# One core, two decoder layers: the feed-forward's 22 tiles in four groups (4, 4, 6, 8) in place of three (6, 8, 8), and weight sums issued in other stages

## The chip, the core and the metric

The program runs on one core of one Trainium2 chip, in one launch. The metric is the device time of that launch in microseconds. TensorE multiplies, VectorE (DVE) and ScalarE (ACT) prepare operands and empty PSUM, GpSimd (POOL) computes a few rows and issues accumulating DMAs, SyncE (SP) issues the loads of the weights.

## The reference, cut to what matters

Two layers on 592 tokens (a prompt of 528, and 8 samples of 8). Each layer is a mixer, a layer norm, a gated feed-forward with a causal convolution of width 3, and a layer norm. The change concerns the feed-forward:

```python
def _conv_ffn(x, buf, w_up, conv_w, conv_b, w_down):
    u, v = jnp.split(x @ w_up, 2, axis=-1)
    uc, new_buf = _causal_dwconv(u, buf, conv_w, conv_b)
    h = jax.nn.gelu(uc.astype(jnp.float32)) * v.astype(jnp.float32)
    return h.astype(x.dtype) @ w_down, new_buf.astype(buf.dtype)
...
    for layer in range(DEPTH):
        if layer % 2 == 0:
            m, s_ret, s_hgrn = _mixer_ret_hgrn(x, pos, segments, s_ret, s_hgrn, layer, p)
        else:
            m, h_lru, buf_lru = _mixer_rglru(x, h_lru, buf_lru, p)
        x = _layernorm(DEEPNORM_ALPHA * x + m, ...)
        f, nb = _conv_ffn(x, buf_ffn[layer], ...)
        x = _layernorm(DEEPNORM_ALPHA * x + f, ...)
```

D_MODEL is 1024 (8 tiles of 128) and D_FF is 2816 (22 tiles of 128), all in float32.

## The kernel before, in words

**Products.** Channels lie on the partitions and tokens on the columns. Every float32 operand is held as a high and a low part, and each 128 x 128 block of a weight takes three matmuls on a half of the tokens (`products`: high by high, high by low, low by high; lines 773 to 775), 296 columns wide in layer 0 and 290 or 288 in layer 1. A unit is one output tile's weights. An up-projection unit (u or v of one feed-forward tile) takes 8 blocks x 2 halves x 3 = 48 matmuls; a down-projection unit takes 6 matmuls for each tile of its group.

**Groups.** The 22 tiles of a feed-forward are worked off in groups (`GROUPS`): the tiles of a group are made one after another, and then eight down units (d0 to d7, one for each output tile) add the group's part to Y. `ffn_order` writes this order. The first `SINGLE` tiles are made one at a time, as unit u and unit v. From there on, two tiles are made together (`pair_of_tiles`): for each of u and v, seven half-sized products of sums of weights and sums of inputs take the place of eight, so that the u or the v of two tiles takes 7 x 4 x 3 = 84 matmuls. A block of four units (a and b for u, p and q for v) makes the two tiles.

**Sums of weights.** They are made in DRAM (`weight_sums`) by `sum_step`: POOL issues eight DMAs in a chain for each group that holds pairs, four of them plain and four accumulating, each behind the landing of the one before. Before the change there are two such groups in a layer, of 8 pair units each, 2048 KB a step. The two of layer 0 are made in the first stage (one step of each after each of the eight heads), the two of layer 1 behind the layer norms numbered 1 and 2 (0 is the one after layer 0's mixer, 3 the last).

**Sums of inputs.** `input_sums(k)` (DVE), their high parts (ACT) and their low parts (DVE) for k = 0 to 3 stand behind the tiles j = 1 to 4.

**The stream of weights.** SP loads the units in order into four buffers `raw` (a pair unit needs two loads, and waits for its group's sums). ACT copies the high part (line 1149, `weights_hi`), DVE subtracts it to make the low part (line 1621, `weights_lo`); each of these has four places. Which unit is prepared in which step is written out (`weights_at`, `block_of_pairs`). SP may refill a `raw` buffer when its low part is made. SP, ACT and DVE each take their work in program order, so that one late load holds what stands behind it.

**PSUM.** Two accumulators alternate between units. A down unit may begin when `add_tile` on DVE (line 1841 where the tile is scaled by alpha, line 1843 otherwise) has added what its accumulator held to Y. A gated tile h is finished by DVE and ACT: rows of the last product, the gate, the high part on ACT, the low part on DVE (`h_lo`); a down unit waits for each h tile in the order in which it reads them.

**The recurrence's rates.** `lambda_rows` (lines 2137 to 2151) computes a few numbers for layer 1's mixer with 27 small DVE instructions; in the kernel before they stand behind the first down unit's `add_tile` of layer 0's first group.

Of the kernel before, what the change touches and what calls it, by code (L numbers as in the profile page):

```python
# [23 lines left out]
P = 128  # L24
# [14 lines left out]
FT = DFF // P  # L39
GROUPS = [6, 8, 8]  # L40
ALPHA = float((2.0 * 2) ** 0.25)
# [19 lines left out]

SINGLE = 6
SUM_STEPS = [(0, "a21", False), (1, "a11", False), (0, "a22", True), (1, "a21", True),
# [29 lines left out]
def mixer_order():  # L93

    order = [("r", 0), ("r", 1)]
    for m in range(2, KT, 2):
# [20 lines left out]
            ("output", -1), ("sample", 1), ("mean", 1), ("moment", 3), ("steps", 3), ("norm", 5)]  # L117
R_LAST = {"sample": 0, "mean": 0, "moment": 2, "steps": 2, "norm": 4}


# [57 lines left out]
def wid(u):  # L178

    return (T - off(u)) // 2  # L180
# [9 lines left out]
PER_LAYER = len(PAIRS) // 2  # L190
PER_GROUP = PER_LAYER // (len(GROUPS) - 1)
RAWS = 4
# [140 lines left out]
def trunk(nc, xT, xP, weights, gates, params, consts, tables, s_ret, s_hgrn, yT, ret_out, hgrn_out, small_out):  # L333
    with ExitStack() as ctx:
# [264 lines left out]
        def _(sp):  # L599
# [6 lines left out]
            def load_weights(u, i):  # L606
# [10 lines left out]
                n = PAIRS.index(u - second(u))  # L617
                sp.wait_ge(w_sums[n // PER_GROUP], 16 * len(SUM_STEPS))
                if second(u):
# [43 lines left out]
        def _(pool):  # L663
# [14 lines left out]
            def sum_step(group, step):  # L678

                first, last = slice(0, HALF), slice(HALF, 2 * HALF)  # L680
                n = group * PER_GROUP
                units = weights[PAIRS[n]:PAIRS[n] + 2 * PER_GROUP].rearrange("(n t) p c -> t p n c", t=2)
                sums = W_SUMS[n:n + PER_GROUP].rearrange("n p c -> p n c")
                to, source, add = SUM_STEPS[step]
                source = {"a11": units[0][:, :, first], "a12": units[0][:, :, last], "a21": units[1][:, :, first],
                          "a22": units[1][:, :, last], "s1": sums[:, :, 0:HALF],
                          "s2": sums[:, :, 2 * HALF:3 * HALF]}[source]
                if step:
                    pool.wait_ge(w_sums[group], 16 * step)
                dst = sums[:, :, to * HALF:to * HALF + HALF]  # L690
                if add:
                    pool.dma_start(dst, source, accum_op=ALU.add).then_inc(w_sums[group], 16)
                else:
                    pool.dma_start(dst, source).then_inc(w_sums[group], 16)
# [6 lines left out]
            for n in range(2 * HEADS):  # L701
# [4 lines left out]
                if n + 2 < 2 * HEADS:  # L706
                    pool.wait_ge(st_out, 32 * (n + 1))
                    load_states(n + 2)
                for group in range(2):
                    sum_step(group, n)  # L710
# [22 lines left out]
            for ln in range(3):  # L733
# [16 lines left out]
                for m in range(KT):  # L750
                    low_row(ln, 1, m)
                if ln:
                    for step in range(len(SUM_STEPS)):
                        sum_step(1 + ln, step)
            for i in range(3):
# [14 lines left out]
        def _(pe):  # L770
# [6 lines left out]
            def gemm(u, hi, lo, k_ready=None, k0=0, both=False, side=None, per=1):  # L777
# [3 lines left out]
                for k in range(n):  # L781
# [19 lines left out]
                    if side:  # L801
                        side(u, k)
                        if both:
                            side(u + 1, k)

            def half_product(u, half, k, hi, lo, signal=None, third=None, norm=None):
# [271 lines left out]
            def ffn(layer):  # L1078
                ub = U_FFN0 if layer == 0 else U_FFN1
                for i, (kind, j, g, first) in enumerate(FFN):  # L1080
# [6 lines left out]
                    elif i > N_FFN - 4:  # L1087
                        pass
                    elif kind == "d":
                        gemm(ub + i, hhi, hlo, h_lo, FT * layer + first)  # L1090
                    elif i == 0:
# [41 lines left out]
        def _(act):  # L1133
# [204 lines left out]
            def ffn(layer):  # L1338
# [88 lines left out]
                for i, (kind, j, g, first) in enumerate(FFN):  # L1427
# [40 lines left out]
                    else:  # L1468
                        if layer == 0 and g == 0 and j == 0:
                            done(act.activation(lam[:, 0:KT], par("lru_lambda", 0, KT), ACT.Abs))  # L1470
# [135 lines left out]
        def _(dve):  # L1606
# [357 lines left out]
            def ffn(layer):  # L1964
# [127 lines left out]
                for i, (kind, j, g, first) in enumerate(FFN):  # L2092
# [33 lines left out]
                    elif kind == "d":  # L2126
                        add_tile(u, j, g == 0, 2 * layer + 1 if g == len(GROUPS) - 1 else None)
                        if layer == 0 and g == 0 and j == 0:
                            lambda_rows()
# [274 lines left out]
```

## Time and profile before

| what | value |
|---|---|
| median of 3 runs | 1366.58 us (1365.96 to 1368.08) |
| the profiled execution's own time | 1366.96 us |
| its span, first to last instruction | 1365.2 us |
| TensorE busy in the span | 1347.3 us, 99%, 9900 matmuls |
| VectorE busy | 952.8 us, 70% |
| ScalarE busy | 723.0 us, 53% |
| GpSimd busy (DMA issues not counted) | 137.7 us, 10% |
| granted TensorE clock | 0.997 of full |

A matmul's row has a length of about 300 ns, since the fill and the drain are in it, while the next one starts some 135 ns later. So the time of a stretch is read from starts, or from a count of matmuls in a window, never from the sum of lengths. The clock at full grant is the 2.4 GHz level. The sequencers' rows (SPq) mark when a load is issued, not when it lands.

### The profile page before, as it was taken

The page shows a single profiled execution, that of the slowest core. Times are in us where ns is not written, and L with a number is a line of the kernel's source. Part 1 is how long each engine was busy: PE and PEld are TensorE (multiplying, and loading weights), DVE is VectorE, ACT ScalarE, POOL GpSimd, SP SyncE. Part 2 cuts the span into 40 slices and gives each one's busy share as a digit, 9 for nine tenths or more (in the row PEclk, how much of TensorE's full clock was granted, in tenths as well). Part 3 has the DMA queues.
Part 4 walks back from the last instruction along what each step waited for, and adds up shares of the span by engine and source line. Part 5 has one row for each costly group of instructions (what it writes and reads, how often), then busy time and mean ns, then how long its engine had stood idle before and what let it go on. Part 6 is the DMA issues. An engine that isn't in the chain of part 4 may idle for free.

```text
span 1365.2 us, 24924 instructions
## 1 busy us (share of the span) xinstructions
PE 1347.3 (99%) x9900; PEld 1319.2 (97%) x9900; DVE 952.8 (70%) x1499; ACT 723.0 (53%) x1137; POOL 137.7 (10%) x146
## 2 busy tenths in 40 slices
PE   9999999999999999999999999999999999999996
PEld 8999998999999999999999999999999999999996
DVE  6656665665887568835886778888784688358865
ACT  5443634454674256623673578646652466246734
POOL 0020111101310000000000420123300000000002
PEclk9999999999999999999999999999999999999998
DMA  8185597859622345523554268752598955235512
GB/s 322 58 263 173 126 229 210 224 152 305 149 65 74 90 133 169 171 78 116 163 170 139 63 202 218 201 136 94 185 201 216 255 169 177 80 115 163 171 62 86
DMA packets 80899, 217.49 MB, mean 159 GB/s; under 512 B 6928, under 2 KB 9232, under 8 KB 80528
## 3 DMA queue, kind: packets, MB, share of 16 engines
q1 hardware_dynamic: 52560, 138.83, 31.7%
q0 software_dynamic: 27648, 76.03, 23.1%
q8 instruction: 78, 1.28, 0.4%
q10 hardware_dynamic: 576, 1.05, 0.2%
q14 instruction: 37, 0.30, 0.1%
HBM read 208.25 MB, written 74.74 MB: 207 GB/s over the span
## 4 chain that ended last, share of the span: by engine, by line
PE 87%; DVE 7%; ACT 3%; DMA 1%; issue 1%; SPq 0%; DVEq 0%; ACTq 0%
PE PS L773 27%; PE PS L774 26%; PE PS L775 26%; DMA raw<-weights 1%; PE PS L981 1%; DVE Y L1916 1%; PE PS L911 1%; DVE Y L1904 1%; PE PS L934 1%; PE PS L974 1%; DVE S L2245 1%; PE PS L953 1%; PE PS L1115 0%; DVE wlo L1621 0%; PE PS L957 0%
## 5 line engine op out<-in xcount | busy, mean ns | idle before, releaser
L773 PE MATMUL PS<-xhi,whi 128*128 128x296 f32 (+1 forms) x1536 | 469.6, 306 | 1.1 <-DVE wlo L1627 0.9
L774 PE MATMUL PS<-xlo,whi 128*128 128x296 f32 (+1 forms) x1536 | 458.1, 298 | 0.0
L775 PE MATMUL PS<-xhi,wlo 128*128 128x296 f32 (+1 forms) x1536 | 457.9, 298 | 0.0
L1149 ACT ACTIVATE whi<-raw 128x1024 fp32r<-128x1024 f32 (+2 forms) x256 | 253.8, 994 | 200.5 <-PE PS L775 192.4
L1621 DVE TENSOR_TENSOR wlo<-raw,whi 128x1024 fp32r<-128x1024 f32 (+2 forms) x256 | 294.2, 1152 | 66.1 <-ACT whi L1149 56.7
L773 PEld LDWEIGHTS PS<-xhi,whi 128*128 128x128 f32 x1536 | 290.3, 189 | 5.4 <-issue 2.2
L774 PEld LDWEIGHTS PS<-xlo,whi 128*128 128x128 f32 x1536 | 290.9, 189 | 1.3
L775 PEld LDWEIGHTS PS<-xhi,wlo 128*128 128x128 f32 x1536 | 289.8, 189 | 0.0
L773 PE MATMUL PS<-hhi,whi 128*128 128x296 f32 (+2 forms) x864 | 258.1, 299 | 0.4 <-DVE Y L1841 0.4
L774 PE MATMUL PS<-hlo,whi 128*128 128x296 f32 (+2 forms) x864 | 256.9, 297 | 0.0
L775 PE MATMUL PS<-hhi,wlo 128*128 128x296 f32 (+2 forms) x864 | 256.3, 297 | 0.0
L773 PEld LDWEIGHTS PS<-hhi,whi 128*128 128x128 f32 x864 | 162.7, 188 | 1.5 <-issue 0.8
L774 PEld LDWEIGHTS PS<-hlo,whi 128*128 128x128 f32 x864 | 162.6, 188 | 0.4
L775 PEld LDWEIGHTS PS<-hhi,wlo 128*128 128x128 f32 x864 | 162.6, 188 | 0.0
L775 PE MATMUL PS<-XT,wlo 128*128 128x296 f32 (+1 forms) x512 | 152.6, 298 | 0.0
L773 PE MATMUL PS<-XT,whi 128*128 128x296 f32 (+1 forms) x512 | 151.9, 297 | 0.0
L774 PE MATMUL PS<-XT,whi 128*128 128x296 f32 (+1 forms) x512 | 151.6, 296 | 0.0
L774 PEld LDWEIGHTS PS<-XT,whi 128*128 128x128 f32 x512 | 96.7, 189 | 0.0
L773 PEld LDWEIGHTS PS<-XT,whi 128*128 128x128 f32 x512 | 96.6, 189 | 0.0
L775 PEld LDWEIGHTS PS<-XT,wlo 128*128 128x128 f32 x512 | 96.3, 188 | 0.0
L725 POOL TENSOR_TENSOR S<-S,Y 128x296 f32<-128x296 f32 (+2 forms) x12 | 9.9, 821 | 707.2 <-DVE Y L1871 660.5
L1843 DVE TENSOR_TENSOR Y<-PS,Y 128x592 f32<-128x592 f32 (+1 forms) x24 | 18.4, 766 | 77.4 <-PE PS L775 77.4
(283 smaller groups left out, 1662.8 us busy)
## 6 DMA issues: line engine op xcount, KB each, us to landing
raw<-weights SPq DMA_DIRECT2D x118, 512.0 KB, 4.4
weight_sums<-weights POOLq DMA_DIRECT2D x24, 2048.0 KB, 16.8
raw<-weights SPq DMA_DIRECT2D x96, 256.0 KB, 3.4
weight_sums<-weight_sums POOLq DMA_DIRECT2D x8, 2048.0 KB, 11.1
raw<-weight_sums SPq DMA_DIRECT2D x64, 256.0 KB, 3.4
raw<-weight_sums SPq DMA_DIRECT2D x32, 512.0 KB, 4.1
raw<-weights SPq DMA_DIRECT2D x16, 384.0 KB, 3.2
Y<-xP SPq DMA_DIRECT2D x8, 296.0 KB, 7.3
```

The source lines that it names most:

```text
L773: pe.matmul(dst, wh, h, start=first, stop=False, skip_group_check=onto)
L774: pe.matmul(dst, wh, lo, start=False, stop=False, skip_group_check=onto)
L775: return pe.matmul(dst, wl, h, start=False, stop=last, skip_group_check=onto)
L911: mm = pe.matmul(out, s(KK, c * P, c * P + P), queries, start=True, stop=True)
L934: mm = pe.matmul(SC[:, b * P:b * P + P], kT[0:w, b, :], v[0:w, b, :], start=True, stop=True)
L953: mm = pe.matmul(OT[:, a:a + P], v[:, PLACE[b], :], s(at, a, a + P), start=True, stop=(b == 0))
L974: mm = pe.matmul(OT[:, 512 * c:512 * c + 512], kT[r:r + 32, BLK, :], VX[r:r + 32, :, :].rearrange("p b v -> p (b v)"), start=True, stop=Tr ...
L981: mm = pe.matmul(PS[:, 4 + half, 0:HT], const("mean_h"), s(row, half * HT, half * HT + HT), start=True, stop=True)
L1149: act.activation(high(u, i)[:, 0:n], raw_of(u, i), ACT.Copy).then_inc(w_hi, 1)
L1621: tt(low(u, i)[:, 0:n], raw_of(u, i), high(u, i)[:, 0:n].bitcast(F32), ALU.subtract).then_inc(w_lo, 1)
L1843: done(tt(y, a, y, ALU.add), free[u % 2], u // 2 + 1)
L1904: done(tt(y, y, over_rows(4 + half, n), ALU.subtract))
```

## The change

`GROUPS` becomes 4, 4, 6, 8 and `SINGLE` 4, so that tiles 4 to 21 are made in pairs: nine blocks in a layer where there were eight, and 32 down units where there were 24. The groups with pairs are now of 4, 6 and 8 pair units, six groups in all. The first two down units of each group are interleaved (`two_down_tiles`): both take all but the last one (first group) or two h tiles, then both take the rest. The steps of the weight sums are dealt out anew: the first seven steps of the groups 0 and 1 in the heads' stage, their eighth behind layer norm 0; groups 2 and 3 and half of 4 after the first two pair products of layer 0; the rest behind the layer norms 1 and 2. The fourth of the input sums moves behind the down units d1, d2 and d3 of the first group, and `lambda_rows` behind d0 of layer 0's third group.

```diff
-GROUPS = [6, 8, 8]
+GROUPS = [4, 4, 6, 8]
...
-SINGLE = 6
+SINGLE = 4
...
+ALL_STEPS = range(len(SUM_STEPS))
+SUMS_BEHIND = [[(0, 7), (1, 7)],
+               [(4, step) for step in ALL_STEPS[4:]] + [(5, step) for step in ALL_STEPS[:2]],
+               [(5, step) for step in ALL_STEPS[2:]]]
+SUMS_BEHIND_PAIRS = [(2, step) for step in ALL_STEPS] + [(3, step) for step in ALL_STEPS] + [(4, step) for step in ALL_STEPS[:4]]
...
-PER_GROUP = PER_LAYER // (len(GROUPS) - 1)
+GROUP_OF = [layer * (len(GROUPS) - 1) + FFN[u - base][2] - 1 for layer, base in enumerate((U_FFN0, U_FFN1))
+            for u in PAIRS if base <= u < base + N_FFN]
...
-                sp.wait_ge(w_sums[n // PER_GROUP], 16 * len(SUM_STEPS))
+                sp.wait_ge(w_sums[GROUP_OF[n]], 16 * len(SUM_STEPS))
...
-                for group in range(2):
+                for group in range(2 if n < 2 * HEADS - 1 else 0):
                     sum_step(group, n)
...
-                if ln:
-                    for step in range(len(SUM_STEPS)):
-                        sum_step(1 + ln, step)
+                for group, step in SUMS_BEHIND[ln]:
+                    sum_step(group, step)
+                if ln == 0:
+                    pool.wait_ge(prod, 2 * PRODUCTS)
+                    for group, step in SUMS_BEHIND_PAIRS:
+                        sum_step(group, step)
...
+            def two_down_tiles(u, late, k0):
+
+                n = unit_tiles(u)
+                for ks in (range(n - late), range(n - late, n)):
+                    for i in range(2):
+                        for k in ks:
+                            pe.wait_ge(h_lo, k0 + k + 1)
+                            cols = slice(k * P, k * P + P)
+                            if k == 0:
+                                weights_ready(pe, u + i)
+                                pe.wait_ge(free[(u + i) % 2], (u + i) // 2)
+                            for half in range(2):
+                                t = span(half, off(u + i))
+                                mm = products(acc[(u + i) % 2][:, half, 0:wid(u + i)], high(u + i)[:, cols],
+                                              low(u + i)[:, cols], hhi[:, k, t], hlo[:, k, t], k == 0, k == n - 1)
+                            if k == n - 1:
+                                mm.then_inc(full[(u + i) % 2], 1)
...
+                    elif kind == "d" and j == 0:
+                        two_down_tiles(ub + i, 2 if g else 1, FT * layer + first)
                     elif kind == "d":
-                        gemm(ub + i, hhi, hlo, h_lo, FT * layer + first)
+                        if j > 1:
+                            gemm(ub + i, hhi, hlo)
...
-                        if layer == 0 and g == 0 and j == 0:
+                        if g == 0 and j == 2:
+                            input_sums_hi(KT // 2 - 1)
+                        if layer == 0 and g == 2 and j == 0:
...
-                        if layer == 0 and g == 0 and j == 0:
+                        if g == 0 and j == 1:
+                            input_sums(KT // 2 - 1)
+                        elif g == 0 and j == 3:
+                            input_sums_lo(KT // 2 - 1)
+                        if layer == 0 and g == 2 and j == 0:
                             lambda_rows()
```

How DVE's instructions stand around `lambda_rows`. Before the change they follow the first `add_tile` (L1841) of layer 0's first down units:

```order
L1621 TENSOR_TENSOR wlo<-raw,whi 128x768 [waits weights_hi,h_lo_ready]
L1841 SCALAR_TENSOR_TENSOR Y<-Y,PS 128x592 [waits acc0_full]
L2137 TENSOR_SCALAR lam<-lam 128x8 [waits lambda_exp,acc0_free]
L2138 RECIPROCAL lam<-lam 128x8 [waits dve_step]
L2139 TENSOR_TENSOR lam<-lam 128x8 [waits dve_step]
```

After the change they follow the first `add_tile` (now L1876) of the third group, which also has down units of six tiles; behind them come the low part of d3's weights and d1's `add_tile`, which frees the accumulator for d3:

```order
L1654 TENSOR_TENSOR wlo<-raw,whi 128x768 [waits weights_hi,h_lo_ready]
L1876 TENSOR_TENSOR Y<-PS,Y 128x592 [waits acc0_full]
L2174 TENSOR_SCALAR lam<-lam 128x8 [waits lambda_exp,acc0_free]
L2175 RECIPROCAL lam<-lam 128x8 [waits dve_step]
```

```order
L2188 TENSOR_SCALAR lam<-W 128x16 [waits dve_step]
L1654 TENSOR_TENSOR wlo<-raw,whi 128x768 [waits weights_hi,half_biases_ready]
L1876 TENSOR_TENSOR Y<-PS,Y 128x592 [waits acc1_full]
L1654 TENSOR_TENSOR wlo<-raw,whi 128x768 [waits weights_hi,acc1_free]
L1876 TENSOR_TENSOR Y<-PS,Y 128x592 [waits acc0_full]
```

The neighbours on DVE are the same; what moved is that TensorE now runs d0 and d1 interleaved ahead of this place. On POOL, the steps that now stand between the layer norms 0 and 1 are these (the middle number of the shape is the number of pair units):

```order
L701 DMA weight_sums<-weights 128x8x512 [waits weight_sums_of_group2]
L699 DMA weight_sums<-weights 128x8x512 [waits weight_sums_of_group2] x2
L701 DMA weight_sums<-weight_sums 128x8x512 [waits weight_sums_of_group2]
L699 DMA weight_sums<-weights 128x8x512 [waits weight_sums_of_group2]
L701 DMA weight_sums<-weight_sums 128x8x512 [waits weight_sums_of_group2]
L699 DMA weight_sums<-weights 128x8x512 [waits weight_sums_of_group2]
L701 DMA weight_sums<-weights 128x4x512
L701 DMA weight_sums<-weights 128x4x512 [waits weight_sums_of_group3]
```

L701 is a plain step and L699 an accumulating one. Before the change no step stands there.

## Rows read from the trace of the kernel before

**Rows 1.** The page: busy time of the engines (us, share, instructions); granted clock in 40 slices.
```profile
PE 1347.3 (99%) x9900; PEld 1319.2 (97%) x9900; DVE 952.8 (70%) x1499; ACT 723.0 (53%) x1137; POOL 137.7 (10%) x146
...
PEclk9999999999999999999999999999999999999998
```

**Rows 2.** TensorE's waits: line, releaser, us in total, times, longest.
```profile
PE PS L773 <- DVE Y L1841: 1.0, 3, 0.6
PE PS L773 <- DVE wlo L1627: 0.9, 1, 0.9
```

**Rows 3.** Windows: stretch, us, PE busy (matmuls begun or running), clock, DMA share, GB/s.
```profile
388.96:447.87 58.91, 58.91 (x435) 1.00 0.25 74
447.87:487.19 39.32, 39.32 (x291) 1.00 0.36 107
487.19:578.33 91.14, 91.14 (x675) 1.00 0.53 157
...
973.62:1031.16 57.54, 57.54 (x434) 1.00 0.89 242
...
1069.28:1159.29 90.01, 90.01 (x674) 1.00 0.64 185
```

**Rows 4.** DVE's timeline, layer 0's d0 and d1: start, us, engine, line, op [idle before].
```profile
452.97 0.77 DVE L1841 SCALAR_TENSOR_TENSOR Y<-Y,PS 128x592 f32<-128x592 f32 x1 [0.94 <-PE PS L775]
...
460.12 0.77 DVE L1841 SCALAR_TENSOR_TENSOR Y<-Y,PS 128x592 f32<-128x592 f32 x1
```

**Rows 5.** TensorE and DVE, timeline, behind two interleaved units of layer 0's mixer.
```profile
325.65 0.30 PE L775 MATMUL PS<-hhi,wlo 128*128 128x296 f32 x1
326.16 0.37 PE L773 MATMUL PS<-hhi,whi 128*128 128x296 f32 x1 [0.21 <-DVE Y L1841]
...
325.25 0.77 DVE L1841 SCALAR_TENSOR_TENSOR Y<-Y,PS 128x592 f32<-128x592 f32 x1 [1.04 <-PE PS L775]
```

**Rows 6.** DVE's timeline behind tile 3 (both layers), and a low part 512 wide.
```profile
420.92 1.22 DVE L1621 TENSOR_TENSOR wlo<-raw,whi 128x1024 fp32r<-128x1024 f32 x1
...
424.61 0.22 DVE L2121 TENSOR_TENSOR S<-PS,S 128x64 f32<-128x64 f32 x1
...
1008.60 0.22 DVE L2121 TENSOR_TENSOR S<-PS,S 128x64 f32<-128x64 f32 x1
...
488.20 0.69 DVE L1621 TENSOR_TENSOR wlo<-raw,whi 128x512 fp32r<-128x512 f32 x1
```

**Rows 7.** ACT, DVE and TensorE, timeline, in front of layer norm 0.
```profile
340.23 1.06 ACT L1149 ACTIVATE xhi<-raw 128x1024 fp32r<-128x1024 f32 x1 [4.57 <-DMA raw<-weights]
...
342.47 0.77 DVE L1841 SCALAR_TENSOR_TENSOR Y<-Y,PS 128x592 f32<-128x592 f32 x1
...
343.38 0.37 PE L773 MATMUL PS<-hhi,xhi 128*128 128x296 f32 x1 [0.61 <-DVE Y L1841]
```

**Rows 8.** DVE's timeline behind the pairs of a group: two h tiles' low parts.
```profile
580.29 1.65 DVE L2043 TENSOR_TENSOR hlo<-S,hhi 128x592 fp32r<-128x592 f32 x2
```

**Rows 9.** POOL's last sum step; DMA in 1067 to 1088; last two lines: the page's.
```profile
1066.43 1.52 POOL L692 DMA_DIRECT2D weight_sums<-weights  x1 [9.20 <-DMA weight_sums<-weight_sums]
...
q1 hardware_dynamic: 1514, 3.25, 43.6%
...
weight_sums<-weights POOLq DMA_DIRECT2D x1, 2048.0 KB, 21.8
raw<-weights SPq DMA_DIRECT2D x5, 256.0 KB, 7.1
...
weight_sums<-weights POOLq DMA_DIRECT2D x24, 2048.0 KB, 16.8
raw<-weights SPq DMA_DIRECT2D x96, 256.0 KB, 3.4
```

**Rows 10.** SP: first load of a pair block behind six-tile units; POOL: start at layer norm 1.
```profile
461.90 0.33 SPq L628 DMA_DIRECT2D raw<-weights  x1
...
766.15 0.82 POOL L725 TENSOR_TENSOR S<-S,Y 128x296 f32<-128x296 f32 x1 [381.77 <-DVE Y L1871]
```

More of the change, by code:

```diff
@@ L680, in sum_step @@
                 first, last = slice(0, HALF), slice(HALF, 2 * HALF)
-                n = group * PER_GROUP
-                units = weights[PAIRS[n]:PAIRS[n] + 2 * PER_GROUP].rearrange("(n t) p c -> t p n c", t=2)
-                sums = W_SUMS[n:n + PER_GROUP].rearrange("n p c -> p n c")
+                n, count = GROUP_OF.index(group), GROUP_OF.count(group)
+                units = weights[PAIRS[n]:PAIRS[n] + 2 * count].rearrange("(n t) p c -> t p n c", t=2)
+                sums = W_SUMS[n:n + count].rearrange("n p c -> p n c")
                 to, source, add = SUM_STEPS[step]
```

## The prediction

> **What bounds the kernel now.** I read the page first: TensorE is busy 99% of the span at the 2.4 GHz level in all but the last slice [rows 1]. Then its waits: of the 18 us in which it is idle, the list of waits names only a handful, each under 2 us, and of the kind that concerns this change there are 1.0 and 0.9 us in all [rows 2]. In the feed-forwards the windows show it busy for their whole length [rows 3], and the timeline has no pause between two products there. So the feed-forwards are bound by the number of matmuls, and every other engine matters only where it becomes late. That makes two kinds of term: matmuls saved, and new waits at places that had none.
>
> **Matmuls.** In layer 0, nine single units (432 matmuls; the count in the row has three more that were still running) take 58.91 us, 6.546 each. Four blocks of pairs (672 matmuls) take 91.14, 22.79 a block. In layer 1 the same are 57.54/9 = 6.393 and 90.01/4 = 22.50 [rows 3]. The change turns two single tiles (four units) of each layer into one block: 26.18 - 22.79 = 3.40 and 25.57 - 22.50 = 3.07. **-6.5 us.** The down units have the same matmuls as before in all (8 x 22 tiles), only cut into 32 units for 24; six-tile units run at 39.32/288 = 136.5 ns a matmul and the single units at 136.4 [rows 3], so a unit's start costs nothing.
>
> The rows show 136 ns from start to start at 296 columns. The Trainium skill ("TensorE: Matmul & The Clock Gate", Part 1) gives N / 2.4 GHz plus about 2.5 ns for back-to-back matmuls, an estimate of 126 ns. By it the term would be -6.0; the trace disagrees, and I go by the rows.
>
> **What pays for the smaller groups.** DVE gets 16 more `add_tile`s of 0.77 us, ACT and DVE six more copies of 1024 columns each (a block prepares seven half units for u and v each, against four for single tiles). These 20 us of DVE work lie beside TensorE: DVE is busy 70%, and they fall into stretches in which TensorE has 3.3 us for a four-tile down unit (24 x 136.5 ns) while DVE needs 0.77 plus 0.69 for the low part. They cost nothing as long as nothing is late. So I looked at each place where something is later than before relative to TensorE.
>
> **lambda_rows.** Before, d0's `add_tile` begins at 452.97, the 27 small instructions, d3's low part and d1's `add_tile` follow, and that last one ends at 460.12 + 0.77 = 460.89, that is 7.92 us after the first began [rows 4]. DVE began 0.2 after d0 was full (447.87 + 4.92 = 452.79 [rows 3]), and TensorE begins 0.14 after a release (326.02 to 326.16 [rows 5]), so d3 may start 0.2 + 7.92 + 0.14 = 8.26 us after d0 is full. Before, d1 and d2 of 4.92 us each lay between, 9.8 us: 1.6 to spare. Now d1 is all but two tiles done when d0 is full. Only 12 matmuls (1.64) and d2 (4.92) are left, 6.56 us. The third group's down units are of six tiles as well, and the instructions behind are the same. TensorE waits 8.26 - 6.56 = **+1.7 us**, in layer 0 alone. ACT's part of it is early enough (d0 lasts longer now).
>
> **d2 behind d0 in the first group.** There only one tile is left for last, so d0 is full 0.8 us ahead of d1, and d2 needs d0's accumulator after those six matmuls. This case is in the trace: the first two units of the output projection are interleaved in the same way, and TensorE's start-to-start there is 0.51 instead of 0.14, with DVE's 0.77 as releaser [rows 5]: 0.37. Twice: **+0.7 us.** In the other groups two tiles are left, 1.64 us, and 0.2 + 0.77 + 0.14 = 1.1 fits.
>
> **d1 behind v3.** Two interleaved units also need both accumulators sooner: d1 begins after three tiles of d0, 2.46 us (layer 1: 2.38), instead of a whole unit of 4.9. v3's accumulator is free when DVE's last gate instruction ends. Tile 3 carries input sums, and there that end is 424.83, 3.14 us after the unit's (388.96 + 5 x 6.546 = 421.69 [rows 3]); in layer 1 it is 1008.82, 3.23 after 973.62 + 5 x 6.393 = 1005.59 [rows 3, 6]. The low part in between shrinks from 1.22 to 0.69 [rows 6]. With the 0.14 that gives 2.75 and 2.84 against 2.46 and 2.38: 0.3 + 0.46, **+0.8 us**. Bounds: 0 and, without the narrower low part, 1.8.
>
> **Behind the pairs of a four-tile group** only four down tiles' halves (3.28 us) hide the last two h tiles, where six (4.9) did. In the trace the two low parts run from 580.29 to 581.94 [rows 8]; the first is ready 2.8 us and the second 3.6 us after TensorE's end at 578.33 [rows 3], against needs at 3.28 and 4.10. With 0.14 it fits by 0.3. I take 0, with 1 us as the upper end for both layers together, should DVE be late there.
>
> **Layer norm 0.** Before, a load of weights that landed at 340.2 kept ACT idle for 4.57 us. DVE's `add_tile` stood behind that load's low part and started only at 342.47, and TensorE began a unit at 343.38, 0.77 later than a product's pace of 0.135 allows (its row counts 0.61 as idle) [rows 7]. The load stood behind five loads of x rows while POOL's two last steps of 2048 KB, which the change moves behind the layer norm, were moving. Without them I expect it 1 us or more earlier: **-0.8 us**, bounds -0.8 and 0.
>
> **Sum:** -6.5 + 1.7 + 0.7 + 0.8 - 0.8 = -4.1 (-4.0 before rounding). The profiled execution took 1366.96, 0.4 more than the median of 1366.58. Its sum gives 1362.9, and against the median I predict **1362.5 us**, 0.3% less.
>
> **Weight sums beside the pairs.** This is the doubtful cover. The sums of groups 2, 3 and 4 now run while TensorE works on pairs, when SP's queue alone keeps the DMA engines busy to 0.53 [rows 3]. The trace has 21 us of this overlap, in layer 1: the last accumulating step took 21.8 us, SP's loads of 256 KB landed in 7.1 us where the page's median is 3.4, SP's queue held 43.6% of the engines and moved 3.25 MB in 21 us, 155 GB/s [rows 9] against 157 needed [rows 3]. TensorE did not pause. So the overlap is at the edge, and a step's 20 us are borne by what is prepared ahead. Between two accumulating steps stands a plain one of about 10 us (9.20 waited plus the issue [rows 9]) in which it catches up, except once, where both lie mostly on down units. I take 0.
>
> **Are the sums in time?** Group 2's eight steps take four times 10.1 and four times 16.8 to 21.8 [rows 9], 108 to 128 us. By the terms above the first two pair products end near 471, so they land by 579 to 599. Tile 14's pairs start near 627, and SP issues their first load some 25 us ahead (461.90 for 487.19 [rows 10]), at 602. It fits, barely. POOL ends its list near 710 (at worst 780, if the smaller steps were no shorter) and is wanted at layer norm 1, near 762 (766.15 before, less the sum [rows 10]).
>
> **The rivals.**
> A. *The new waits stay covered* (DVE's order gives more than I see). Then only -6.5 - 0.8 are left: 1359.3 us. For it: no pause in 790 us of feed-forward. Against it: rows 4 and 5 carry the two main waits. 0.15.
> B. *SP's queue falls behind beside the sums; slower than before.* The accumulating steps cover some 110 us of pair stages in layer 0. If SP's queue got half of the engines where it needs 0.53, each us would lose 6%: +6.5, hence 1369. It decides from landings of about 9 us on: a buffer is refilled every four loads, 11.4 us, of which ACT and DVE take 1.06 and 1.22 [rows 6, 7] with a short wait between. The trace has 7.1 [rows 9], and nothing shows what a second such step does. 0.09.
> The Trainium skill ("DMA: Bandwidth & Descriptors", Queues, rings and completion order) says that each DMA engine takes turns between the queues with work, a packet at a time, whatever waits on them. By that rule SP's loads get no precedence; rows 9 agree.
> C. *Group 2's sums or POOL are late.* SP, then ACT, DVE and TensorE wait in turn for tile 14, or layer norm 1 does. Steps 5 us longer than the longest would put it 20 us past 602, against about 15 of reserve: +5, hence 1367.5. 0.05.
> D. *The boundaries cost about double* (h tiles of the four-tile groups, lateness on DVE from late loads, no gain at layer norm 0): +2 to +3, hence 1365. 0.15.
> The forecast keeps 0.56.
>
> **How the numbers follow.** A measurement of this kernel tells 0.2%, 2.7 us, from no change: the border is 1363.8. Faster holds A and 0.51 of the forecast's 0.56: 0.66. Within 0.2% are the forecast's rest, D and a part of C: 0.22. Slower: B and the rest of C, 0.12. The range from 1359.5 to 1367.0 spans the forecast with its bounds, D and most of A, and leaves out B and half of C.
>
> **What would show it.** Right: TensorE has 9852 matmuls; blocks take 22.8 and 22.5 us; TensorE waits once for 1.7 us for `add_tile` in the third group of layer 0, twice for 0.2 to 0.4 in front of d2, twice in front of d1 in the first groups, and no longer at 343. Wrong: a wait on weights' low parts inside the pair blocks of layer 0 (B), SP idle for the sums of group 2 (C), or waits on h tiles behind the second group (D).

## The result, and the profile after

| what | before | after |
|---|---|---|
| median of 19 runs each | 1366.93 us (1365.96 to 1368.19) | 1372.98 us (1368.13 to 1382.21) |
| ratio, 95% interval | | 1.0044 (1.0035 to 1.0054) |
| the profiled execution's own time | 1366.96 us | 1373.03 us |
| its span | 1365.2 us | 1371.1 us |

The change makes the kernel 0.4% slower, where I had forecast 0.3% faster. The time lies outside the range, 6 us above its upper end, and beyond rival B's 1369 too. The profile is of an execution close to the median, so its pauses can be read as the usual ones.

The page of the changed kernel, against [rows 1] and the end of [rows 9]:

```profile
PE 1345.0 (98%) x9852; PEld 1313.2 (96%) x9852; DVE 980.5 (72%) x1555; ACT 734.4 (54%) x1165; POOL 152.3 (11%) x162
...
q1 hardware_dynamic: 57168, 141.98, 31.8%
q0 software_dynamic: 30976, 84.41, 25.9%
...
raw<-weights SPq DMA_DIRECT2D x140, 256.0 KB, 4.3
```

TensorE has the 9852 matmuls that the change promises, 48 fewer. They should have taken 6.5 us of busy time away, and only 2.3 are gone: a matmul's row is 300 ns long where the next one starts after 136, and the first row behind a pause is longer still, so a part of each pause counts as busy. Idle time went from 17.9 us to 26.1. The median landing of SP's loads of 256 KB went from 3.4 to 4.3 us over the whole run, which looks harmless. A median over 140 loads hides the few that matter (13 of them in the stretch that is looked at below).

TensorE's waits, against [rows 2]:

```profile
PE PS L783 <- DVE S L2048: 3.0, 4, 1.5
PE PS L783 <- ACT S L1404: 2.5, 4, 1.0
PE PS L783 <- DVE wlo L1660: 2.0, 2, 1.6
PE PS L783 <- DVE Y L1876: 1.6, 1, 1.6
...
PE PS L783 <- DVE S L2154: 0.3, 1, 0.3
```

The last two rows are waits that the prediction named: `lambda_rows`, and d1 behind v3 in layer 1. Those in front of d2 are too short for a row of their own, and so is d1's in layer 0; they are read from starts below. The third row lies in the first 10 us of the program, with the first products of all. The first two are new and were not named: instructions that empty the accumulators of pairs (L2048 on DVE, L1404 on ACT). They are not slow themselves; they stand behind something. The windows say where. They begin and end with the first matmuls of units or blocks, as in [rows 3]; the last two are of layer 1. Columns: stretch, us, busy time and count of PE, PEld, DVE, ACT and POOL, clock, DMA share, GB/s:

```profile
421.61:448.55 26.94, 26.67 (x195) 26.24 (x194) 19.62 (x28) 9.07 (x14) 0.00 (x0) 1.00 0.43 129
520.34:591.96 71.62, 69.13 (x506) 68.41 (x505) 54.44 (x83) 43.08 (x73) 5.64 (x5) 1.00 0.98 270
633.06:725.90 92.84, 91.86 (x674) 91.20 (x673) 74.22 (x112) 60.73 (x100) 8.50 (x8) 1.00 0.94 262
1035.78:1084.15 48.37, 46.35 (x338) 45.20 (x337) 36.56 (x56) 28.19 (x50) 2.42 (x2) 1.00 0.78 225
1110.38:1177.89 67.51, 67.51 (x506) 67.51 (x505) 55.17 (x85) 43.65 (x73) 0.00 (x0) 1.00 0.52 162
```

The clock is at full grant in all of them, so it has no part in this. The last row is the measure: three blocks of pairs of layer 1 with no sums beside them take 67.51 us, 22.50 each, as before. The fourth holds two blocks and takes 48.37 instead of 45.0. The second holds three blocks of layer 0 and takes 71.62 instead of 3 x 22.79 = 68.4, the third four and takes 92.84 instead of 91.1 (from 91.14 in [rows 3]). In these three the DMA engines are busy to 0.78 to 0.98, where the pairs alone took 0.53 before [rows 3]. Taken block by block from the starts of the matmuls, the pauses inside blocks add up to 5.0 us in layer 0 and 3.4 in layer 1, where the interleaved d0 and d1 of the second group, with DVE late, lose another 0.8 behind the fourth window: **9.2 us** in all. My sum without them was -4.0, which gives +5.2. Measured between the two profiled executions is +6.1, and 0.8 of that is a later start of the first products, ahead of everything that the change touches (the third row of waits).

### One pause, followed back

The pause of 1.8 us at 566, in the second of the three blocks from 520 to 592 us, engine by engine (timelines of ACT, DVE and TensorE):

```profile
563.14 1.06 ACT L1180 ACTIVATE whi<-raw 128x1024 fp32r<-128x1024 f32 x1 [3.24 <-DMA raw<-weight_sums]
...
564.30 1.23 DVE L1654 TENSOR_TENSOR wlo<-raw,whi 128x1024 fp32r<-128x1024 f32 x1 [2.43 <-ACT whi L1180]
565.45 0.45 DVE L2048 TENSOR_TENSOR S<-S,PS 128x296 f32<-128x296 f32 x1
...
565.96 0.41 PE L783 MATMUL PS<-XT,whi 128*128 128x296 f32 x1 [1.53 <-DVE S L2048]
...
567.92 1.06 ACT L1180 ACTIVATE whi<-raw 128x1024 fp32r<-128x1024 f32 x1 [2.38 <-PE PS L785]
```

ACT waits 3.24 us for a load, which landed 9.7 us after SP had issued it at 553.41. DVE waits for ACT's high part, 2.43 us. The instruction that frees the accumulator stands behind the low part in DVE's order, and TensorE waits for that. So the list of waits names a short instruction that empties an accumulator, where the cause is a late load three steps up. The next high part starts at 567.92. Its row names TensorE, whose product ended at 567.86; its load landed at the same moment, 12.8 us after SP had issued it at 555.03, so that either alone would have held it. What ACT does behind a late high part (L1404, which empties an accumulator) is the second row of the list of waits.

What ended ACT's idle time before its high parts, over blocks of pairs of layer 0. Changed kernel, 520 to 592 us:

```profile
  DMA raw<-weight_sums: 6.4, 3
  DMA raw<-weights: 6.2, 4
  PE PS L785: 4.8, 4
```

The kernel before, 520 to 577 us, has one row:

```profile
  PE PS L775: 9.8, 12
```

Before, ACT waited for TensorE alone, that is for a place to write to: it was ahead. Now more than half of its waiting is for loads. And the DMA of the same stretch of the changed kernel:

```profile
q0 software_dynamic: 3475, 9.08, 55.5%
q1 hardware_dynamic: 4615, 10.24, 42.7%
...
weight_sums<-weight_sums POOLq DMA_DIRECT2D x2, 2048.0 KB, 11.5
weight_sums<-weights POOLq DMA_DIRECT2D x2, 2048.0 KB, 20.3
raw<-weights SPq DMA_DIRECT2D x13, 256.0 KB, 8.2
...
raw<-weight_sums SPq DMA_DIRECT2D x8, 256.0 KB, 8.7
```

SP's queue (q1) holds 42.7% of the engines, against 43.6% in the stretch from which I argued [rows 9], so that reading was right. It moves 10.24 MB in 72 us, 142 GB/s, against the 157 that pairs need [rows 3]: 10% short. The landings of 8.2 to 8.7 us are near the 9 from which rival B was said to decide, and as a median, so that half are longer.

The mean share hides how a step begins. The accumulating step issued at 549.69, in two stretches of the changed kernel's DMA, 553.5 to 556.5 and 557 to 565 us (queue, packets, MB, share; SP's loads issued in it, count, KB, median landing):

```profile
q0 software_dynamic: 257, 0.53, 107.9%
...
raw<-weight_sums SPq DMA_DIRECT2D x2, 256.0 KB, 10.1
raw<-weights SPq DMA_DIRECT2D x1, 256.0 KB, 12.8
...
q0 software_dynamic: 489, 1.00, 72.1%
q1 hardware_dynamic: 471, 0.87, 35.9%
```

For 3 us SP's queue moved no packet at all, though four of its loads were outstanding by 555.1, among them the two of the pause above; without the sums a load's first packets move within 1 us of its issue (after_no_sums, issued at 549.47). From then on the queues moved about as many packets each. The other steps beside pairs begin with 1 to 3 such us as well, plain ones too (541 to 543.5: 233 packets against none), and when a step's last packets are through, SP's queue has the engines alone for some 2 us (549.7 to 552: 382 packets against none). The Trainium skill ("DMA: Bandwidth & Descriptors", Queues, rings and completion order) lets each DMA engine take turns between the queues by packet; 557 to 565 us agrees, with 489 packets against 471, the first 3 us of the step do not, and no run here shows why.

POOL's timeline shows the plain step in which SP was to catch up:

```profile
538.46 0.92 POOL L701 DMA_DIRECT2D weight_sums<-weight_sums  x1 [21.14 <-DMA weight_sums<-weights]
549.69 1.52 POOL L699 DMA_DIRECT2D weight_sums<-weights  x1 [10.31 <-DMA weight_sums<-weight_sums]
```

It took 10.9 us as expected (issued 538.46, landed 549.32), and in the 11 us from 538 to 549 the software queue held 56.2% and SP's 29.7% of the engines. SP's 29.7% goes with two things in the trace: 2.5 us in which its queue moved nothing beside the step, and before them some 1.5 us in which it had little left to move, since it issued no load between 535.33 and 540.47. The step is shorter than an accumulating one; there was no rest in it.

### The other terms

`lambda_rows` in the third group of layer 0, against [rows 4] (DVE, then TensorE, timeline):

```profile
600.35 0.77 DVE L1876 TENSOR_TENSOR Y<-PS,Y 128x592 f32<-128x592 f32 x1 [2.51 <-PE PS L785]
...
607.49 0.77 DVE L1876 TENSOR_TENSOR Y<-PS,Y 128x592 f32<-128x592 f32 x1
...
608.40 0.37 PE L783 MATMUL PS<-hhi,whi 128*128 128x296 f32 x1 [1.55 <-DVE Y L1876]
```

From the first `add_tile` to the end of the second it is 7.91 us, 7.92 before, and TensorE starts d3 1.7 us late (start to start 6.61 from d2, where 4.91 is its pace). The interleaved d0 and d1 of the first group with the waits around them: the first window above holds these and d2 to d7, 192 matmuls, 26.94 us, where 192 x 0.1364 = 26.19, so +0.75. From the starts it is 0.37 in front of d1 and 0.38 in front of d2; in layer 1 it is 0.51 and 0.38, together 0.89. Forecast were 0.3 + 0.37 = 0.67 and 0.46 + 0.37 = 0.83. In front of layer norm 0, the 192 matmuls behind the two interleaved units (from 326.97; 326.16 before) take 26.23 us instead of 27.08, and ACT no longer waits for a load ([rows 7] had 4.57 us):

```profile
335.40 2.01 ACT L1180 ACTIVATE xhi<-raw 128x1024 fp32r<-128x1024 f32 x2
```

### The profile page after: what moved, and what is told of

It reads as the page before. It is cut to its first block, busy times and chain, and to the rows that moved or that the text cites. A ratio compares the mean times of both kernels' runs of the same rounds, so it can differ in the third digit from the quotient of the medians.

```text
span 1371.1 us, 25074 instructions
## 1 busy us (share of the span) xinstructions
PE 1345.0 (98%) x9852; PEld 1313.2 (96%) x9852; DVE 980.5 (72%) x1555; ACT 734.4 (54%) x1165; POOL 152.3 (11%) x162
## 4 chain that ended last, share of the span: by engine, by line
PE 80%; DVE 10%; DMA 4%; ACT 4%; issue 2%; DVEq 0%; SPq 0%; ACTq 0%
PE PS L783 25%; PE PS L785 24%; PE PS L784 24%; DMA raw<-weights 3%; DMA raw<-weight_sums 2%; PE PS L1009 1%; DVE wlo L1654 1%; DVE Y L1949 1%; PE PS L939 1%; DVE Y L1937 1%; PE PS L962 1%; PE PS L1002 1%; DVE S L2282 1%; ACT whi L1180 1%; PE PS L981 1%
## 5 line engine op out<-in xcount | busy, mean ns | idle before, releaser
L783 PE MATMUL PS<-xhi,whi 128*128 128x296 f32 (+1 forms) x1456 | 445.9, 306 | 2.2 <-DVE wlo L1660 2.0
L785 PE MATMUL PS<-xhi,wlo 128*128 128x296 f32 (+1 forms) x1456 | 434.2, 298 | 0.0
L784 PE MATMUL PS<-xlo,whi 128*128 128x296 f32 (+1 forms) x1456 | 434.2, 298 | 0.0
L783 PEld LDWEIGHTS PS<-xhi,whi 128*128 128x128 f32 x1456 | 275.2, 189 | 6.3 <-issue 2.2
L784 PEld LDWEIGHTS PS<-xlo,whi 128*128 128x128 f32 x1456 | 275.8, 189 | 1.4
L785 PEld LDWEIGHTS PS<-xhi,wlo 128*128 128x128 f32 x1456 | 274.7, 189 | 0.0
L783 PE MATMUL PS<-XT,whi 128*128 128x296 f32 (+1 forms) x576 | 172.1, 299 | 5.5 <-DVE S L2048 3.0
L785 PE MATMUL PS<-XT,wlo 128*128 128x296 f32 (+1 forms) x576 | 171.7, 298 | 0.0
L784 PE MATMUL PS<-XT,whi 128*128 128x296 f32 (+1 forms) x576 | 170.6, 296 | 0.0
L783 PEld LDWEIGHTS PS<-XT,whi 128*128 128x128 f32 x576 | 108.7, 189 | 8.0 <-DVE S L2048 4.6
L784 PEld LDWEIGHTS PS<-XT,whi 128*128 128x128 f32 x576 | 108.8, 189 | 0.0
L1876 DVE TENSOR_TENSOR Y<-PS,Y 128x592 f32<-128x592 f32 (+1 forms) x40 | 30.6, 765 | 65.8 <-PE PS L785 65.6
L2122 DVE SCALAR_TENSOR_TENSOR S<-S,W 128x608 f32<-128x608 f32 (+1 forms) x72 | 60.8, 844 | 2.7 <-ACT S L1390 0.8
```

The source lines that it names most:

```text
L783: pe.matmul(dst, wh, h, start=first, stop=False, skip_group_check=onto)
L784: pe.matmul(dst, wh, lo, start=False, stop=False, skip_group_check=onto)
L785: return pe.matmul(dst, wl, h, start=False, stop=last, skip_group_check=onto)
L1876: done(tt(y, a, y, ALU.add), free[u % 2], u // 2 + 1)
L2122: done(stt(y, r[:, q:q + m], par("ffn_conv_w", (layer * FW + q) * FT + j), y, ALU.mult, ALU.add), conv if q == FW - 1 else None)
```

## The experiments

Theory T: everything in the feed-forwards is as costed, and the whole surprise, some 10 us, is the weight sums beside pairs. Rivals: the rest lies in the interleaved down units and `lambda_rows` (U), or in accumulating DMAs alone rather than in any bulk transfer (V, as part of T). Each run is compared with runs of the kernel before on the same chip, whose medians go from 1366.63 to 1367.06 us, so that a difference between two runs below is uncertain by some 0.4 us from the chip alone; the labels are those of the kernels.

### 1 and 2: both kernels without any sums (after_no_sums, before_no_sums)

```diff
+LEFT_OUT = (0, 1, 2, 3, 4, 5)
...
+                made = GROUP_OF[n] not in LEFT_OUT
+                sums = W_SUMS[n] if made else weights[u]
+                if made:
+                    sp.wait_ge(w_sums[GROUP_OF[n]], 16 * len(SUM_STEPS))
...
+                if group in LEFT_OUT:
+                    return
```

SP loads as many bytes as ever, from the weights; POOL issues none of the steps.

> The changed kernel without any of the DMAs that make the weight sums; the pair units load as many bytes as before, from the weights themselves, so that the pairs' products are of other numbers. Theory (traffic): the 9.2 us of pauses inside the pair blocks and behind the second group of layer 1 come from SP's loads landing late beside POOL's sum steps. Then all of them go and only the forecast's own terms are left: 1366.9 - 6.5 + 1.7 + 0.7 + 0.7 - 0.8 = 1362.7 us, with runs within 1 us of each other, loads landing in about 4 us, blocks of 22.8 and 22.5 us, and the 1.7 us wait in front of d3 of the third group still there. Rival (own work): the pauses come from the extra work on ACT and DVE and from the shorter lead of the smaller groups; then they stay and the time is 1370 or more.

> The kernel before without the DMAs of the weight sums, in the same way (the pairs' products are of other numbers). Traffic: only the 0.8 us pause in front of layer norm 0 goes, 1366.1 us. If it is unchanged, that pause is not the sums' work. Either theory of the new pauses says the same of this kernel; it is the base for the one above.

Measured: the changed kernel 1362.53 us, ratio 0.9963 (0.9949 to 0.9977); the kernel before 1366.17, ratio 0.9991 (0.9982 to 1.0001). So the sums cost the kernel before under 1 us, and the changed one 10.5. Between the two without sums the difference is 3.6 us, where the sum gives 3.3 (-6.5 + 1.7 + 0.7 + 0.8; the gain in front of layer norm 0 came from sums moved away there, and without sums both kernels have it). TensorE's waits of the changed kernel without sums:

```profile
PE PS L789 <- DVE Y L1882: 1.6, 1, 1.6
...
PE PS L789 <- DVE S L2160: 0.3, 1, 0.3
```

The waits for emptied accumulators inside blocks are gone; what is left in the feed-forwards is what the prediction named. That decides for T against U: the down units' waits stand in this kernel as well, and it is still over 4 us faster than the kernel before.

### 3 and 4: which layer (no_sums_234, no_sums_5)

```diff
+LEFT_OUT = (2, 3, 4)
```
```diff
+LEFT_OUT = (5,)
```

The first removes the steps that run beside pairs in layer 0 (and group 4's), the second those of the last group, whose steps reach into layer 1.

> The changed kernel without the sums of groups 2, 3 and 4 (the ones that run beside layer 0's pairs, and half of group 4 behind layer norm 1); their pair units load the weights in their place. Traffic: layer 0's pauses (5.0 us in the profile) go, layer 1's (4.2) stay: about 1367.5 us. Own work: nothing changes in layer 0, 1372 to 1373.

> The changed kernel without the sums of group 5 alone (behind the layer norms 1 and 2); its pair units load the weights in their place. Traffic: layer 1's pauses (4.2 us) go, layer 0's 5.0 stay: about 1368 us. Own work: layer 1 keeps its pauses, 1372 to 1373.

Measured: 1365.44 us, ratio 0.9986 (0.9977 to 0.9996), and 1370.67, ratio 1.0024 (1.0006 to 1.0041). Against the changed kernel's 1372.98 these are 7.5 and 2.3 us less, together 9.8 of the 10.5. In no_sums_234 layer 0 has no pause in a block, and the first block of layer 1 loses 3.8 us. In no_sums_5 it is the other way round: layer 1 is clean, the blocks of layer 0 lose 7.0 us, nearly all of it in eight places. The size of a layer's loss varies from run to run (5.0 us in the changed kernel's profile), and I expected both numbers some 2 to 3 us off from where they came out, in opposite directions: more of the loss is layer 0's than the one profile shows.

### 5 and 6: the waits of the down units (lambda_later, not_interleaved)

Both start from after_no_sums, so that no late load covers what is measured.

```diff
-                        if layer == 0 and g == 2 and j == 0:
+                        if layer == 0 and g == 2 and j == 3:
```
```diff
-                    elif kind == "d" and j == 0:
-                        two_down_tiles(ub + i, 2 if g else 1, FT * layer + first)
                     elif kind == "d":
-                        if j > 1:
-                            gemm(ub + i, hhi, hlo)
+                        gemm(ub + i, hhi, hlo, h_lo, FT * layer + first)
```

> The changed kernel without the weight sums' DMAs (1362.5 us), and the 27 small instructions of the recurrence's rates behind the third group's d3 instead of its d0. If the wait in front of d3 is worth what the working says (8.26 us of DVE against 6.56 of cover), it goes and nothing takes its place, since two whole down units (9.8 us) lie behind the new place: 1362.5 - 1.7 = 1360.8 us. If something else of the group holds TensorE there (late weights, ACT), the time stays at 1362.5.

> The changed kernel without the weight sums' DMAs, and with each group's d0 and d1 one after the other, as before the change. By the working: behind tile 3 TensorE waits for h's low part, ready 4.45 us after v3, with 2.46 of cover: +2.0 in place of 0.65, in both layers: +2.7. Behind the four-tile group of pairs the h tiles are ready 2.94 us after the end and wanted after 1.64: +1.3 in both layers: +2.6. The 1.7 us in the third group go. Sum 1362.5 + 2.7 + 2.6 - 1.7 = 1366.1 us. Rival: the interleaving buys nothing and costs its two waits; then 1362.5 - 1.7 - 1.3 = 1359.5.

Measured: 1360.75 us, ratio 0.9952 (0.9935 to 0.9968), and 1366.62, ratio 0.9999 (0.999 to 1.0008). `lambda_rows` behind d3 saves 1.8 us (1.5 when each kernel is set against the kernel before on its own chip), against the 1.7 of the trace. Without the interleaving the kernel loses 4.1 us, and the list of waits says at what:

```profile
PE PS L789 <- DVE hlo L2160: 3.4, 2, 1.8
PE PS L789 <- DVE hlo L2079: 2.4, 2, 1.3
```

The low parts of the last h tiles: behind a group of four tiles a down unit is too short to hide them. The interleaving that I had costed at +1.5 is in fact worth 4 here, near the 3.6 expected before this run. In the prediction I had never priced what it replaces.

### 7: the kernel before with its sums beside pairs (before_beside_pairs)

```diff
-                if ln:
-                    for step in range(len(SUM_STEPS)):
-                        sum_step(1 + ln, step)
+                if ln == 0:
+                    pool.wait_ge(prod, 2 * PRODUCTS)
+                    for group in (2, 3):
+                        for step in range(len(SUM_STEPS)):
+                            sum_step(group, step)
```

No group, unit or down tile is changed: only the sixteen steps for layer 1 run where the change puts its own.

> The kernel before (groups 6, 8, 8), with one thing of the change: the sums of layer 1's two groups are issued after the first two pair products of layer 0 instead of behind the layer norms 1 and 2. Traffic: the overlap alone makes pauses in layer 0's blocks, over more of them than in the changed kernel, 5 to 8 us: 1372 to 1375 us, and single runs several us apart. Rival: the overlap hurts only because the four-tile groups leave less prepared ahead; then the kernel before bears it, 1367 to 1368.

Measured: 1376.01 us, ratio 1.0067 (1.0046 to 1.0088), that is +9.2 us, above the 5 to 8 expected. The placement alone makes the old kernel slower by about as much as the changed one loses. Its waits at pairs are of the same kinds, for an accumulator emptied by DVE or by ACT, and one for a low part, and its DMA in 660 to 715 us shows nearly the same shares:

```profile
PE PS L775 <- DVE S L2017: 2.5, 3, 1.7
PE PS L775 <- ACT S L1375: 2.3, 2, 1.3
...
PE PS L775 <- DVE wlo L1623: 0.7, 1, 0.7
```
```profile
q0 software_dynamic: 2778, 6.96, 59.2%
q1 hardware_dynamic: 3634, 7.68, 40.8%
```

### 8: the changed kernel with its sums elsewhere (sums_off_pairs)

The whole computation, with the steps dealt out so that nearly all of them run beside heads, single tiles, down units and the layers' ends:

```diff
+SUMS_BEHIND_HEADS = [[], [0, 1, 2], [], [3], [], [4, 5], [], []]
+SUMS_BEHIND = [[(0, 7), (1, 7), (2, 6), (2, 7)],
+               [(4, step) for step in ALL_STEPS[3:]] + [(5, step) for step in ALL_STEPS[:4]],
+               [(5, step) for step in ALL_STEPS[4:]]]
+SUMS_BEHIND_GROUPS = [(4, [(3, step) for step in ALL_STEPS[:3]]), (10, [(3, step) for step in ALL_STEPS[3:]]),
+                      (18, [(4, step) for step in ALL_STEPS[:3]])]
...
+                    for count, steps_then in SUMS_BEHIND_GROUPS:
+                        pool.wait_ge(prod, count * PRODUCTS)
+                        for group, step in steps_then:
+                            sum_step(group, step)
```

> The changed kernel with all its sums, dealt out so that hardly any step runs beside pairs: groups 0 to 2 behind the heads and layer norm 0, group 3 behind the pair products of the second and third groups of layer 0 (while their down units run), group 4 behind layer 0's last pairs and layer norm 1, group 5 behind layer norms 1 and 2. Traffic: 1362.7 us as without any sums, perhaps 0.5 more where steps reach into the next block, and runs within 1 us of each other. Rival: the sums cost the same wherever they stand in the feed-forward or the mixers; then 1367 and more.

Measured: 1363.82 us, ratio 0.9976 (0.9967 to 0.9985), with no pause in any block of pairs. It is 9.2 us under the changed kernel with the same work, and 1.3 above the one without sums. Expected were 0 to 0.5 above; where the rest lies is open.

### 9: is it the adding, or any bulk transfer? (plain_only)

```diff
-                    pool.dma_start(dst, source, accum_op=ALU.add).then_inc(w_sums[group], 16)
+                    pool.dma_start(dst, source).then_inc(w_sums[group], 16)
```

> The changed kernel with its sum steps where they are, but all of them plain: the four accumulating ones of each group copy and do not add, so that the sums are of other numbers. They then last some 10 us in place of 17 to 22 for 2048 KB. If plain steps press on SP's queue as much as accumulating ones (theory: the queue's share counts, not the kind), layer 0's second group of pairs, which they still cover, keeps its pauses of about 3.3 us; the third group keeps little, and layer 1 none, because group 5 is done by then: about 1366 us. Rival: only accumulating steps slow SP's loads; then no pauses, 1362.7.

Measured: 1363.51 us, ratio 0.998 (0.9971 to 0.9989), between what the two theories said, nearer to the rival's 1362.7 than to the 1366 expected. Seven of ten runs lie between 1362.8 and 1364.1, three between 1365.4 and 1367.2, and the profiled one is of the latter, with pauses of 2.3 and 1.9 us in two units. Its DMA in 520 to 560 us:

```profile
q0 software_dynamic: 1746, 6.96, 51.7%
q1 hardware_dynamic: 2594, 5.51, 40.3%
...
weight_sums<-weights POOLq DMA_DIRECT2D x2, 2048.0 KB, 12.5
```

While it runs, a plain step takes nearly as large a share as an accumulating one. It is over in 12.5 us rather than 20, and the whole chain ends sooner. So most of the loss needs the long steps, but a plain step is no rest. How the loss divides between the two kinds in the changed kernel is not settled by this run.

### 10: the best version (sums_off_pairs_lambda)

sums_off_pairs with the edit of lambda_later; it computes everything.

> All sums, dealt out off the pairs (1363.8 us before), and the recurrence's rates behind the third group's d3. The two repairs are independent: 1363.8 - 1.7 = 1362.1 us, 4.8 us under the kernel before.

Measured: **1361.59 us** (1361.16 to 1362.08), ratio 0.9957 (0.9943 to 0.997): faster than both kernels. Its page and waits, and its DMA in 520 to 588 us:

```profile
PE 1342.1 (99%) x9852; PEld 1313.1 (97%) x9852; DVE 981.6 (72%) x1555; ACT 738.0 (54%) x1165; POOL 153.0 (11%) x162
```
```profile
PE PS L788 <- DVE wlo L1665: 1.1, 1, 1.1
...
PE PS L788 <- DVE S L2159: 0.3, 1, 0.3
```
```profile
q1 hardware_dynamic: 4886, 10.96, 52.2%
```

Of the waits only the last is in a feed-forward. SP's queue moves 10.96 MB in 68 us, 161 GB/s, where it got 142 beside the sums.

Two other remedies were not tried: more buffers `raw`, and loads spread over two hardware queues.

## Why the prediction was wrong

**The step that failed** is the one on weight sums beside the pairs: "I take 0". It measures 10.5 us (1372.98 against 1362.53 without sums), 9.2 of them as pauses of TensorE in the changed kernel's profile. Four things were wrong in it.

- *The plain step as a rest.* "Between two accumulating steps stands a plain one of about 10 us in which it catches up." In those 10 us SP's queue had 29.7% of the engines, less than beside an accumulating step. I had read a plain step's duration from rows, and its share from nowhere.
- *A mean share in place of a course in time.* The 43.6% [rows 9] are a mean over 21 us. Its step begins with 3 us of almost nothing for SP, in the trace of the kernel before already (1071.5 to 1074.5 us: 4 packets of SP's queue against 287); in the changed kernel the loads issued from 553.0 to 555.1 us landed 7.5 to 12.8 us later.
- *The stretch that served as evidence.* The 21 us of overlap in the kernel before [rows 9] fall on the first pairs of layer 1, directly behind six-tile down units, where loads of weights land 7 to 9 us ahead of ACT; in the middle of the pair stage they are mostly 4 to 6 us ahead. One step used up that lead: the loads for ACT's instructions at 1085.0 and 1088.54 landed 0.2 and 0.1 us ahead. The trace of the kernel before had a warning that I passed over. One half of a pair unit's weights, issued at 1078.8 beside that step (who waited, and issue to landing):

```profile
  ACT whi L1149: 1.2, 1
...
DMA to landing us min/median/max: 9.7/9.7/9.7
```

The same loads at 1101 to 1135, with no sums beside them:

```profile
DMA to landing us min/median/max: 3.9/3.9/4.0
```

ACT was already waiting. TensorE did not pause; that this was because it was a single step with a reserve in front of it is my reading.
- *Layer 1.* I priced layer 0 alone. With SINGLE = 4 the pairs of layer 1 begin at 1035.78 instead of 1069.28, and the last group's steps end at 1071 instead of 1088: 35 us of overlap and two steps where there were 19 us and one, 4.2 us.

Rival B had the mechanism right (though not its sign: in the changed kernel's blocks TensorE waited for the accumulators emptied behind late low parts, not for the low parts themselves), with SP short by 6% by an even split and 10% as measured, and a border (landings of 9 us) close to the medians of 8.2 to 8.7. The numbers around it, landings of 7.1 against 9 us and 155 against 157 GB/s, left a margin of 1% in rate, and 0.09 was far too small a chance for what such a margin leaves open.

**What held.** Matmuls: blocks of 22.5 us where nothing disturbs them, and 9852 matmuls. `lambda_rows`: +1.7 forecast, 1.7 in the trace, 1.8 by its own run. The interleaved units: 0.75 and 0.89, forecast 0.67 and 0.83. Layer norm 0: -0.85, forecast -0.8. The sum without the failed step, 1362.5, is what the kernel without sums takes (1362.53), though that kernel has no sums in front of anything else either. DVE's extra work is 27.7 us (980.5 against 952.8), not the 20 that I had counted; it cost nothing where no load was late.

**h tiles behind a group of four** (I took 0, with 1 as the upper end): 0 in layer 0, and 0.8 in layer 1 only where DVE was late from late loads. Without sums both are 0.

**Rivals.** A (waits covered) is out, since all its waits are in the trace. C is out: group 2's last step landed at 603.3, later than the 599 I gave it, as its steps took up to 22.4 us; but SP issued the first load that needs it only at 609.28, behind a low part of DVE's, so the reserve held. D is out as a cause, except for the 0.8 above.

## What to carry to other kernels

When bulk transfers are moved beside a stage, ask not whether the engines have room on average but how much the small loads of that stage get while the bulk one runs, how far ahead of use they land there, and for how long it lasts, read in stretches of a few us and not as a mean; one overlap that was survived at the head of a stage says little about its middle. A wait that names a cheap instruction is to be followed back along the order of its engine before it is believed. And a stage that moves earlier meets whatever transfers ran there before: look at both layers.

## What was not expected of the hardware

- A queue of small loads gets 40 to 44% of the DMA engines beside one chain of bulk steps (42.7, 43.6, 40.8 and 40.3% in four stretches), and 29.7% in one plain step's 11 us. But it gets them unevenly: none or nearly none in a step's first 1 to 3 us (no packet in 553.5 to 556.5 us), then as many packets as the bulk queue (471 against 489), then the engines alone. Its loads of 256 KB land in 8.2 us as a median, one in 12.8, instead of 3 to 4. The cause of the first 1 to 3 us is open.
- With the sums beside pairs the times spread: the changed kernel's 19 runs cover 14 us, no_sums_5's ten 1365.9 to 1376.8, and those of the changed kernel without sums beside pairs (runs 1, 8 and 10; 5 to 10 runs each) 0.9 to 2.0.
- A plain step of 2048 KB between two places of DRAM takes 10.4 to 12.5 us, and the accumulating ones of the same size 19.0 to 22.4 beside pairs.
